# The beginning of a two-layer decoder trunk taken tile by tile: order of the first loads, splits and statistics

## The reference, cut to what matters

```
for l in range(DEPTH):
    h = rmsnorm(x, pre_mix_g[l])
    z = h @ w_in[l]                      # q | k | v | u | g
    q = partial_rotary(q, positions)     # needs sin and cos of the angles
    k = partial_rotary(k, positions)
    attn = dilated_mixture_attention(q, k, v)
    uc = causal_dwconv(u, conv_w[l], conv_b[l])
    rec = rg_lru(uc, ...)                # sigmoids, exp, tanh, sqrt, scan
    rec = jax.nn.gelu(g) * rec
    mixed = concat(rmsnorm(attn), rmsnorm(rec))
    x = x + rmsnorm(mixed @ w_out[l], post_mix_g[l])
    h = rmsnorm(x, pre_ffn_g[l])
    x = x + rmsnorm(ffn(h), post_ffn_g[l])
```

## Time and profile before

| | |
|---|---|
| median of 3 runs | 1437.75 us (1437.74 to 1437.78) |
| the profiled execution | 1437.94 us, its span 1436.1 us |
| TensorE busy | 1419.7 us, 99% of the span |
| vector engine busy | 1198.4 us, 83% |
| ScalarE busy | 1037.5 us, 72% |
| moved by DMA | 454.10 MB, mean 316 GB/s |

### The profile page before, as it was taken

How to read it: one execution, slowest core, us unless ns; L and a number is a source line. 1 busy time by engine, 2 the same in 40 slices (tenths; PEclk the granted TensorE clock), 3 DMA queues, 4 the chain that set the end, 5 groups by cost and what they waited for, 6 DMA issues and landing times.

```text
span 1436.1 us, 20676 instructions
## 1 busy us (share of the span) xinstructions
PE 1419.7 (99%) x7000; PEld 1183.5 (82%) x7000; DVE 1198.4 (83%) x1389; ACT 1037.5 (72%) x1287; POOL 23.3 (2%) x17
## 2 busy tenths in 40 slices
PE   9999999999999999999999999999999999999997
PEld 6988888887887888888888888888888888888885
DVE  7877665556877899898898899889989989899996
ACT  6766544455676877877787797787788778777775
POOL 0000000000001200000000000000000000001001
PEclk9999999999999999999999999999999999999999
DMA  9436965544524599999999999999999999999991
GB/s 375 180 131 228 373 232 202 198 176 176 191 105 160 226 421 415 359 401 381 353 404 385 379 383 384 369 367 401 382 355 392 390 371 384 392 375 377 421 382 74
DMA packets 68898, 454.10 MB, mean 316 GB/s; under 512 B 9456, under 2 KB 9712, under 8 KB 17008
## 3 DMA queue, kind: packets, MB, share of 16 engines
q1 hardware_dynamic: 61056, 432.47, 77.6%
q10 hardware_dynamic: 6640, 16.78, 3.2%
q0 software_dynamic: 1152, 4.19, 0.7%
HBM read 438.21 MB, written 15.20 MB: 316 GB/s over the span
## 4 chain that ended last, share of the span: by engine, by line
PE 95%; DVE 2%; issue 1%; ACT 1%; DMA 0%; SPq 0%; DVEq 0%; ACTq 0%
PE psum L515 24%; PE psum L517 24%; PE psum L516 23%; PE psum L595 8%; PE psum L601 4%; PE psum L522 2%; PE psum L523 2%; PE psum L1056 2%; PE psum L1108 1%; PE psum L528 1%; PE psum L642 1%; PE psum L755 0%; PE psum L548 0%; PE psum L696 0%; PE psum L1044 0%
## 5 line engine op out<-in xcount | busy, mean ns | idle before, releaser
L1518 DVE TENSOR_TENSOR w_lo<-ring,w_hi 128x1024 fp32r<-128x1024 f32 x812 | 943.4, 1224 | 50.4 <-ACT w_hi L1171 49.6
L1171 ACT ACTIVATE w_hi<-ring 128x1024 fp32r<-128x1024 f32 x812 | 806.8, 1052 | 55.1 <-PE psum L517 43.1
L515 PE MATMUL psum<-w_hi,hT_both 128*128 128x512 f32 (+1 forms) x976 | 380.0, 389 | 0.0
L517 PE MATMUL psum<-w_hi,hT_both 128*128 128x512 f32 (+1 forms) x976 | 374.0, 383 | 0.0
L516 PE MATMUL psum<-w_lo,hT_both 128*128 128x512 f32 (+1 forms) x976 | 373.2, 382 | 0.0
L515 PE MATMUL psum<-w_hi,act_hi 128*128 128x512 f32 x560 | 218.8, 391 | 0.0
L517 PE MATMUL psum<-w_hi,act_lo 128*128 128x512 f32 x560 | 218.2, 390 | 0.0
L516 PE MATMUL psum<-w_lo,act_hi 128*128 128x512 f32 x560 | 218.2, 390 | 0.0
L517 PEld LDWEIGHTS psum<-w_hi,hT_both 128*128 128x128 f32 x976 | 183.4, 188 | 36.6
L515 PEld LDWEIGHTS psum<-w_hi,hT_both 128*128 128x128 f32 x976 | 183.6, 188 | 34.4
L516 PEld LDWEIGHTS psum<-w_lo,hT_both 128*128 128x128 f32 x976 | 183.8, 188 | 33.9
(11 more groups left out here) (266 smaller groups left out, 935.3 us busy)
## 6 DMA issues: line engine op xcount, KB each, us to landing
ring<-moe_gate SPq DMA_DIRECT2D x112, 1024.0 KB, 7.3
ring<-moe_up SPq DMA_DIRECT2D x112, 1024.0 KB, 7.7
ring<-moe_down SPq DMA_DIRECT2D x112, 1024.0 KB, 7.6
ring<-in_units SPq DMA_DIRECT2D x19, 1024.0 KB, 8.0
ring<-dense_gate SPq DMA_DIRECT2D x14, 1024.0 KB, 4.9
ring<-dense_up SPq DMA_DIRECT2D x14, 1024.0 KB, 4.9
ring<-dense_down SPq DMA_DIRECT2D x14, 1024.0 KB, 4.9
ring<-out_units SPq DMA_DIRECT2D x8, 1024.0 KB, 7.5
```

The costliest lines, as they stand in the source:

```text
L515: pe.matmul(dst, s_hi, m_hi, start=start, stop=False)
L517: return pe.matmul(dst, s_lo, m_hi, start=False, stop=stop)
L1171: act.activation(w_hi[:, h % AHEAD, :], ring[:, n % RING, (h % 2) * HCOLS:(h % 2 + 1) * HCOLS], ACT.Copy).then_inc(hi_ready, 1)
L1518: dve.tensor_tensor(w_lo[:, h % AHEAD, :], ring[:, (h // 2) % RING, (h % 2) * HCOLS:(h % 2 + 1) * HCOLS], w_hi[:, h % AHEAD, :].bitcast(F3 ...
```

## The change

In the order of the streams:

- SyncE: the gain row and the first half unit are issued ahead of x tile 1, which goes between the two half units. The identity moves to ScalarE's DMA queue, ahead of the positions.
- TensorE: one ones-matmul instead of two before and after; the matmuls of tile 0 with both halves of the first unit stand ahead of the transposes of tile 1, with a ones-matmul between the two halves; then tile 1 with both halves; then the second unit as before.
- ScalarE: sum of squares of tile 0, first half's high weights, high parts of tile 0, second half's high weights, and only then the sum of squares and high parts of tile 1.
- The vector engine: tile 0 normalised, low weights 0, low parts of tile 0, low weights 1, tile 1 normalised, low parts of tile 1, low weights 2 and 3, and only then `softplus_start` and `angles`.

```diff
         def _(sync):
             sync.dma_start(xs[:, 0, :], x[0]).then_inc(x_loaded[0], 16)
-            sync.dma_start(xs[:, 1, :], x[1]).then_inc(x_loaded[1], 16)
             sync.dma_start(gain[:, 0, :], gains[0:1].partition_broadcast(P)).then_inc(pre_gain_loaded, 16)
-            sync.dma_start(con[:, 0:P], consts[:, 0:P]).then_inc(ident_loaded, 16)
...
                     sync.dma_start(ring[:, 0, 0:HCOLS], src[:, 0:HCOLS]).then_inc(first_half_loaded, 16)
+                    sync.dma_start(xs[:, 1, :], x[1]).then_inc(x_loaded[1], 16)
                     sync.dma_start(ring[:, 0, HCOLS:UCOLS], src[:, HCOLS:UCOLS]).then_inc(unit_loaded[0], 16)
...
                 if layer == 0:
-                    warm(2, 4)
+                    warm(1, 4)
+                    norm_hi_wait(0, 0, 0)
+                    token_highs(first, 6, 0, 0, 0)
+                    norm_wait(0, PRE_MIX, 0, 0)
+                    token_lows(first, 6, 0, 0, 0)
+                    warm(1, 4)
+                    token_highs(first, 6, 0, 1, 0)
+                    token_lows(first, 6, 0, 1, 0)
                     turn_rows_of(0, 1)
-                    warm(2, 4)
-                    for i in range(2):
+                    norm_hi_wait(0, 0, 1)
+                    token_highs(first, 6, 0, 0, 1)
+                    norm_wait(0, PRE_MIX, 0, 1)
+                    token_lows(first, 6, 0, 0, 1)
+                    token_highs(first, 6, 0, 1, 1)
+                    token_lows(first, 6, 0, 1, 1)
+                    for i in range(1, 2):
...
         def _(act):
+            act.dma_start(con[:, 0:P], consts[:, 0:P]).then_inc(ident_loaded, 16)
             act.dma_start(pos_i[:, :], positions).then_inc(pos_loaded, 16)
...
                 if layer == 0:
-                    for tt in range(TT):
-                        sumsq_x(0, tt)
+                    sumsq_x(0, 0)
+                    keep_up(0, 1)
                     norm_hi(0, 0)
-                    keep_up(0, 1)
+                    keep_up(0, 2)
+                    sumsq_x(0, 1)
                     norm_hi(0, 1)
...
                 if layer == 0:
-                    for tt in range(TT):
-                        normalise(0, tt)
+                    normalise(0, 0)
+                    keep_up(0, 1)
                     norm_lo(0, 0)
-                    keep_up(0, 1)
+                    keep_up(0, 2)
+                    normalise(0, 1)
                     norm_lo(0, 1)
-                    keep_up(first, 2)
+                    keep_up(first, 4)
                     softplus_start()
                     angles()
```

## The result

| | before | changed |
|---|---|---|
| median | 1437.87 us (14 executions) | 1442.84 us (14) |
| lowest to highest | 1437.74 to 1439.08 | 1439.13 to 1443.55 |
| profiled execution: time, span | 1437.94, 1436.1 | 1440.75, 1438.9 |

The ratio is 1.0024, interval 1.0018 to 1.0031: slower by about 3.5 us, which is how far the means lie apart (1441.8 and 1438.2). The medians lie 5.0 us apart, for more than half of the changed kernel's executions are in its upper groups. The executions fall into groups. Before: 9 at 1437.74 to 1437.89 and 5 at 1438.9 to 1439.1. Changed: 4 at 1439.1 to 1439.4, 2 at 1440.8 to 1441.0, one at 1442.4, 7 at 1443.3 to 1443.55. The lowest groups are 1.4 to 1.5 us apart, near the 1.2 that was forecast; the upper groups were not forecast.

A forecast was written before the change was run, and what follows sets the result against it. TensorE, busy 99%, was taken as the bound, with the vector engine's full queue deciding at the second turning of heads. Queue 1.5 us late, chain behind it 1.2: 1437.75 + 1.2 = 1438.95 us, range 1437.2 to 1440.3.

The forecast's parts named there:

- The forecast's chain: From early loads to layer 0's second turning of heads: vector engine 1.5 us late, TensorE 1.75 us ahead, then waiting.
- turning: TensorE's second turning of heads, layer 0: at 70.35 instead of 69.15, after TensorE stands some 2 us.
- TensorE's wait behind the gates: After the gates end at 49.65, TensorE waits for the second GeLU until 50.5: 0.85 us.
- high weights 7: ScalarE's high weights 7, queued behind Sin, come about 1.1 us later because the angles are late.
- The forecast's sum, +1.2: At the second turning of heads: the vector engine's lateness makes the whole kernel 1.2 us slower, median 1438.95.
- those for half 1: First unit's second half lands at 10.5; bounds 10.0 giving +0.7 and 11.3 giving +2.0.
- rival C: TensorE's clock falls after the 2 us gap: 3 us lost, 1442.0; chance 0.06.
- My price for a fall, 3.0 us: After the 2 us gap, slow matmul spacing returns for 6 us, as at the start, losing 3 us.
- The statement that no gap was over 0.6: Kernel before, TensorE between 10 and 69 us: no gap over 0.6 us.
- A: TensorE's whole 1.75 us lead arrives at the end: 1436.0; chance 0.10.
- B: A wash: vector engine's queue late by at most 0.3, the two effects cancel, 1437.75; chance 0.12.
- D: More waits than counted, half 1 pushed back or splits colliding: about 1440.3; chance 0.04.

The follow-up runs named there:

- e12: Changed kernel plus two ones-matmuls each ahead of layer 0's second turning of heads and layer 1's first norm's transposes: 1439.11 to 1439.46 us, ratio 1.0005 to before.
- e3: Changed kernel with tile 1's sum of squares, normalisation and transposes moved earlier: 1437.24 to 1437.55 us in 8 of 11, ratio 0.9996 to before.
- e6: Changed kernel with tile 1's statistics earlier and layer 0's softplus and first rotation later: 1436.22 to 1436.78 us in 7 of 11, ratio 0.9989 to before.
- e7: Kernel before plus twelve linked tiny instructions (about 2.4 us) ahead of softplus on the vector engine: 1439.85 to 1444.35 us, ratio 1.0022 to before.
- e5: Changed kernel run once more, unedited, to profile another execution: 1443.46 us.
- e1: Changed kernel plus two ones-matmuls (1.72 us) ahead of layer 0's second turning of heads: 1439.11 to 1440.56 us, median 1439.36, ratio 1.0010 to before.
- e9: Kernel before plus two ones-matmuls (1.72 us) ahead of the transposes of layer 1's first norm: 1437.50 to 1437.78 us in all 11.
- e2: Changed kernel plus one ones-matmul (0.86 us) ahead of layer 0's second turning of heads: 1439.16 to 1440.48 us, median 1440.25, ratio 1.0012 to before.
- e4: Changed kernel with layer 0's softplus moved behind the g sum and the first rotation later: 1436.8 to 1437.4 us in ten of 11, ratio 0.9992 to before.

## Why the prediction was wrong

**What held.** The forecast's chain held step by step, to some tenths: gain at 6.75 (6.5), transposes at 8.46 (8.4), tile 1's sum of squares at 11.57 (11.5), the vector engine late by 1.64 (1.5), second unit at 18.61 (18.3), u columns at 24.07 (23.8), end of the g sum near 49.5 (49.35), turning at 70.54 (70.35) behind an idle stretch of 2.05 (2). Two terms were off without harm to the sum: TensorE's wait behind the gates was 0.42 (0.85), and high weights 7 came 3.1 us later than before (26.22 for 23.10), where the forecast had 1.1; the vector engine was at softplus then. The forecast's sum, +1.2, measured +1.4 with the clock kept up (e12), by experiments that take the lateness away (e3, e6) and make it elsewhere (e7). Of the bounds, those for half 1 were not needed: it landed near 10.55.

**What failed.** The step is rival C: "by the length it names, these gaps stay below it, and no row of this kernel shows such a fall", and the chance of 0.06 put on it. The 2.05 us stretch brought the clock down in ten of the first 14 executions, by their groups, and in e5; a stretch of 2.07 in another kernel in 7 of 11 (e7). The Trainium skill's page "TensorE: Matmul & The Clock Gate", in "Why this matters for your kernels", names a length of gap from which the clock is lost; the runs with shorter gaps, near 2 us, decide against taking it for a safe bound. My price for a fall, 3.0 us, was the long form (+3.0); the short one is +1.5. With C as likely as not, the forecast would have had two centres, 1439 and 1442, and a chance near one half for slower.

**What I did not look for.** The kernel before has the same thing: the stretch of 1.81 us at 355.8 was in its profile, and 5 of its 14 executions lie 1.2 us high. Its first three, 1437.74 to 1437.78, happened to have none. The statement that no gap was over 0.6 was about the first 69 us only. That trace even has a fall, at its end: TensorE does no work from about 1427.7 on, and the granted clock is 1.00 from 1428 to 1430 and 0.57 from 1430 to 1432.

**Rivals.** A (the lead passes) needed what e6 gives, an early vector engine, and then arrives as 1.5 us. B and D did not occur.

**Open.** Why the fall comes in some executions and not in others, and short in one and long in another, is not settled; nothing here varies it. That the fall comes with the gap is shown (e1, e7, e9, e12). No fall followed the stretches of 1.07 and 1.17 us (e3, e2) in the profiled executions, and none is seen in the groups; every profile also has 1.11 to 1.16 us of idle near 465 us, and the clock holds there. Some falls followed the stretches of 1.8 us and above. How often is open too: with the same stretch of 1.8 us at layer 1's first norm, the upper group has one execution of 11 in e4 and 7 of 11 in e2.

## What to carry to other kernels

A lead on the busiest engine is worth only what the second fullest queue can follow; look for the place downstream where the two meet with no slack, and move work of the second engine out of the way before making the first one faster. Do not put the statistics of a tile behind the split of a weight half that lands later than the tile.

A wait on TensorE is to be priced twice: its own length, and the clock that it may lose. Where a stretch of 2 us cannot be avoided, two matmuls of ones in it cost nothing here and took 3.5 us off the median.

## What was not expected of the hardware

- The granted clock fell to 0.50 after idle stretches of 1.81 and 2.05 us, in part of the executions. In the changed kernel it did so only when TensorE had been busy again for 1 to 1.5 us (busy from 70.5, the fall at 71.5 or 72.0), in e7 as the stretch ended. The clock then stayed at half for most of 72 to 76 us in one execution, through to 78 in another, though the engine was busy 2.00 of every 2 us.
- 2.4 us more on an engine that is busy 83% of the span cost 3.7 us of the median (e7), of which 2.3 are between the lowest groups and the rest the clock.
- The landing of the first broadcast row, issued at the same time, varied by up to 0.3 us between profiles of kernels with the same loads (6.1 us from issue in the kernel before, 5.8 in e7 and e9). The first normalisation is at 7.82 before and at 7.53 in e9, which is the same kernel up to 355 us, and the difference goes through to the turning of heads (69.16 and 68.87) and to the whole execution (1437.94 and 1437.63).
